# Hybrid mLSTM and pooling trunk: sums of z weight quarters of the pool input projection formed in device memory by accumulating DMAs, in place of VectorE's additions

## The reference

```python
def _pool_branch(x, w_in, w_group, scale, w_out):
    proj = x @ w_in                 # 1024x1024 @ 1024x4096
    u = proj[..., :E_B]             # E_B = 2048
    z = proj[..., E_B:]
    ...
    pooled = (jnp.concatenate(means, axis=-1) - uf).astype(x.dtype)   # moving means of u, windows 2, 4, 8, 16
    mixed = jnp.einsum("bsgc,gcd->bsgd", pooled, w_group).reshape(B, S, E_B) * scale
    return (mixed * jax.nn.silu(z)) @ w_out
...
x = _layer_norm(DEEPNORM_ALPHA * x + branch(x), post_ln_g[i], post_ln_b[i])
```

## Time and profile before

| | before |
|---|---|
| median of 3 runs | 1450.5 us (1450.19 to 1453.4) |
| span of the profiled execution | 1451.6 us |
| TensorE busy | 1433.7 us (99%) |
| VectorE busy | 1035.0 us (71%) |
| ScalarE busy | 767.7 us (53%) |
| GpSimd busy | 58.7 us (4%) |
| moved by DMA | 141.99 MB |

### The profile page before, as it was taken

One profiled execution on the slowest core, in us unless ns is written; L12 is line 12 of the kernel. 1 busy time (PEld: TensorE's weight loads), 2 busy tenths in 40 slices (PEclk: granted clock), 3 DMA queues, 4 the chain that ended last, 5 costly groups with the idle time before them and its releaser, 6 DMA issues.

```text
span 1451.6 us, 19237 instructions
## 1 busy us (share of the span) xinstructions
PE 1433.7 (99%) x6680; PEld 1192.7 (82%) x6680; DVE 1035.0 (71%) x1634; ACT 767.7 (53%) x1209; POOL 58.7 (4%) x125
## 2 busy tenths in 40 slices
PE   9999999999999999999999999999999999999997
PEld 7788888888888888888888888878888888888886
DVE  7978878797887879787734133677788777796515
ACT  6876757667576757658633234574444444442201
POOL 2001000000001000000000000000000000000001
PEclk9999999999999999999999999999999999999999
DMA  5022122131222203135473333441222222463121
GB/s 221 24 68 95 52 67 74 49 102 45 98 62 73 73 30 102 59 134 207 126 247 102 91 97 101 138 122 54 80 87 88 74 87 88 136 270 104 42 88 58
DMA packets 67360, 141.99 MB, mean 98 GB/s; under 512 B 6065, under 2 KB 32945, under 8 KB 66625
## 3 DMA queue, kind: packets, MB, share of 16 engines
q1 hardware_dynamic: 67264, 140.77, 29.6%
HBM read 111.32 MB, written 29.43 MB: 97 GB/s over the span
## 4 chain that ended last, share of the span: by engine, by line
PE 92%; ACT 4%; DVE 2%; DMA 1%; issue 1%; SPq 0%; POOL 0%; DVEq 0%; ACTq 0%; POOLq 0%
PE wide L2678 20%; PE wide L2680 20%; PE wide L2679 20%; PE ps_state L2678 3%; PE ps_state L2680 3%; PE ps_state L2679 3%; PE ps_inter L2679 2%; PE ps_inter L2678 2%; PE ps_inter L2680 2%; PE ps_intra L2850 2%; PE ps_state L2856 2%; PE ps_intra L2853 2%; PE ps_intra L2679 1%; PE ps_s L2679 1%; PE ps_intra L2678 1%; PE ps_s L2678 1%
## 5 line engine op out<-in xcount | busy, mean ns | idle before, releaser
L2679 PE MATMUL wide<-xa,inb 128*128 128x512 f32 x576 | 224.5, 390 | 0.0
L2678 PE MATMUL wide<-xb,inb 128*128 128x512 f32 x472 | 189.7, 402 | 0.9
L2680 PE MATMUL wide<-xb,inb 128*128 128x512 f32 x472 | 184.3, 390 | 0.0
L2679 PEld LDWEIGHTS wide<-xa,inb 128*128 128x128 f32 x576 | 108.4, 188 | 19.9
L2679 PE MATMUL wide<-xa,blk 128*128 128x512 f32 x320 | 124.5, 389 | 0.0
L2678 PEld LDWEIGHTS wide<-xb,inb 128*128 128x128 f32 x472 | 88.8, 188 | 20.2 <-issue 3.7
L2680 PEld LDWEIGHTS wide<-xb,inb 128*128 128x128 f32 x472 | 88.6, 188 | 18.9
L2680 PE MATMUL wide<-xb,blk 128*128 128x512 f32 x256 | 99.6, 389 | 0.0
L2678 PE MATMUL wide<-xb,blk 128*128 128x512 f32 x256 | 99.6, 389 | 0.0
L2678 PE MATMUL wide<-xa,inb 128*128 128x512 f32 x208 | 83.3, 400 | 4.2 <-ACT z_buf L1084 2.9
L2680 PE MATMUL wide<-xa,inb 128*128 128x512 f32 x208 | 81.2, 390 | 0.0
(11 more groups left out here) (436 smaller groups left out, 3826.8 us busy)
## 6 DMA issues: line engine op xcount, KB each, us to landing
in_raw<-in_w_in SPq DMA_DIRECT2D x45, 512.0 KB, 3.9
y_heads<-f_buf SPq DMA_DIRECT2D x32, 256.0 KB, 3.3
wm_raw<-in_w_out SPq DMA_DIRECT2D x16, 512.0 KB, 6.4
a_raw<-in_pool_w_z SPq DMA_DIRECT2D x16, 512.0 KB, 3.7
a_raw<-folded SPq DMA_DIRECT2D x16, 512.0 KB, 3.7
y_rows<-zz SPq DMA_DIRECT2D x16, 512.0 KB, 2.7
wo_raw<-in_pool_w_out SPq DMA_DIRECT2D x16, 512.0 KB, 7.7
ym_raw<-y_heads SPq DMA_DIRECT2D x32, 192.0 KB, 2.5
```

What stands on the lines that cost most here:

```text
L2678: pe.matmul(dst, a[0], b[0], start=first, stop=False, skip_group_check=more)
L2679: pe.matmul(dst, a[0], b[1], start=False, stop=False, skip_group_check=more)
L2680: return pe.matmul(dst, a[1], b[0], start=False, stop=last, skip_group_check=more)
```

## The change

The weights of z come in another layout: four parts, each [128, 8, 512] (`by_part` in place of `by_pair`), so that a part of all eight z pairs is one block of 2 MiB. Four arrays `z_sums[7]`, `[6]`, `[3]`, `[5]` of 2 MiB are added in device memory. GpSimd forms them with eight DMAs of its own, `z_step(0)` to `z_step(7)`, one at the end of each head: four plain copies within device memory (steps 0, 2, 4, 6) and four that add a part onto what is there (steps 1, 3, 5, 7). Each waits for the one before (`z_summed`). In the pool layer the 7 z pairs from p = 2 on take their sums from there: SyncE loads them (`load_sum`, four loads of 256 KB a pair) and no longer loads part 2. VectorE's four additions of these pairs go (28 in all); pair 0 and the u pairs keep theirs. The number of the semaphore for the gate weights is changed too (`gw_placed` becomes two more counts of `const_set`), with the same waits.

```diff
+Z_SUMS = (7, 5, 6, 3)
+Z_STEPS = 8
+def summed_on_chip(p):
+    return p % 2 == 1 or p == 0
...
+            def load_sum(p, q):
+                if q == 3:
+                    if p == 2:
+                        sp.wait_ge(added, 4)
+                    sp.wait_ge(blk_lo, AT[p - 2, 3] + 1)
+                else:
+                    sp.wait_ge(prod, AT[p, q] - RING + 1)
+                if p == 2 and q == 3:
+                    sp.wait_ge(z_summed, 16 * Z_STEPS)
+                dst = a_part(p, 2) if q == 3 else blk_sum_at(AT[p, q])
+                src = z_sums[q].rearrange("(c n) f -> c (n f)", n=2)[:, p // 2 * HALF:(p // 2 + 1) * HALF]
+                sp.dma_start(dst, src).then_inc(z_sum_in[q], 16)
...
-            for p in range(PAIRS - 2):
-                load_a(p + 2, 0)
-                if p >= 3 and p % 2:
+            for p in range(PAIRS):
+                if p and p % 2 == 0:
+                    for q in (6, 7, 5):
+                        load_sum(p, q)
+                if p < PAIRS - 2:
+                    load_a(p + 2, 0)
+                    if p % 2 == 0:
+                        load_sum(p + 2, 3)
...
+            def z_step(n):
+
+                part = [p_z[a, :, :, :].rearrange("c (m k) f -> (c m) (k f)", m=2) for a in range(4)]
+                dst, src, adds = ((7, part[0], False), (7, part[2], True), (6, z_sums[7], False), (6, part[3], True),
+                                  (3, z_sums[6], False), (3, part[1], True), (5, part[2], False), (5, part[3], True))[n]
+                if n:
+                    pool.wait_ge(z_summed, 16 * n)
+                if adds:
+                    pool.dma_start(z_sums[dst], src, accum_op=ALU.add, max_dma_last_dim=8192).then_inc(z_summed, 16)
+                else:
+                    pool.dma_start(z_sums[dst], src, max_dma_last_dim=8192).then_inc(z_summed, 16)
...
                 for f in range(2):
                     power(h, f)
+                z_step(h)
...
-                if (p, q) in AT and q == 5 and p + 1 < PAIRS:
+                if q == 5 and p + 1 < PAIRS and summed_on_chip(p + 1):
                     for part in (7, 6, 3):
                         add(p + 1, part)
-                elif q == 1 and p:
+                elif q == 1 and p and summed_on_chip(p):
                     add(p, 5)
```

More of the change, by code:

```diff
@@ L183, in a_loads, with sums_before @@
     return 16 * ((1 if p % 2 else PAIRS_A - 1) + p // 2 + 1)
+def summed_on_chip(p):
+    return p % 2 == 1 or p == 0
+def sums_before(p):
+    return 4 * (p // 2 + 1) if p else 0
 def by_vector(n):
@@ L208, in build @@
     folded = nc.dram_tensor("folded", (P, PAIRS // 2, 2, 2, 4, P), F32, kind="Internal").ap()
+    z_sums = {q: nc.dram_tensor(f"z_sum{q}", (2 * P, 4 * HALF), F32, kind="Internal").ap() for q in Z_SUMS}
     y_heads = nc.dram_tensor("y_heads", (ET, P, S), F32, kind="Internal").ap()
@@ L431, in build @@
         gw_in = sem("gw_in")
-        gw_placed = sem("gw_placed")
+        z_summed = sem("z_summed")
         bias_in = sem("bias_in")
@@ L552, in build @@
         late_in = y_in[4]
+        z_sum_in = dict(zip(Z_SUMS, (xt_in[1], xt_in[2], xt_in[3], xt_in[4])))
         wg_late_in = gw_in
@@ L587, in block_raw @@
             p, q = PRODUCTS[i]
-            return a_part(p, {1: 0, 2: 1, 3: 1, 4: 3}[q]) if q < 5 else blk_sum_at(i)
+            return a_part(p, {1: 0, 2: 1, 3: 1 if summed_on_chip(p) else 2, 4: 3}[q]) if q < 5 else blk_sum_at(i)
         def is_u(p):
@@ L737, in load_a @@
                     sp.wait_ge(blk_lo, AT[p - 2, 4 if j else 3] + 1)
-                src = folded[:, p // 2, j, :, :, :] if p % 2 else p_z[p // 2, :, j, :, :, :]
-                sp.dma_start(a_raw[:, p % 2, 2 * j:2 * j + 2, :],
-                             src.rearrange("c h t f -> c h (t f)")).then_inc(a_in[p % 2][j], 16)
+                parts = slice(2 * j + (j if not summed_on_chip(p) else 0), 2 * j + 2)
+                src = (folded[:, p // 2, j, :, :, :].rearrange("c h t f -> c h (t f)") if p % 2
+                       else p_z[parts, :, p // 2, :].rearrange("a c f -> c a f"))
+                sp.dma_start(a_raw[:, p % 2, parts, :], src).then_inc(a_in[p % 2][j], 16)
+            def load_sum(p, q):
[10 more added lines that the diff above has]
+                sp.dma_start(dst, src).then_inc(z_sum_in[q], 16)
             def store_y(k):
@@ L853, in _ @@
                             load_wm(k)
-            for p in range(PAIRS - 2):
-                load_a(p + 2, 0)
-                if p >= 3 and p % 2:
+            for p in range(PAIRS):
[6 more added lines that the diff above has]
+                        load_sum(p + 2, 3)
+                if 3 <= p < PAIRS - 2 and p % 2:
                     store_y(p - 2)
-                load_a(p + 2, 1)
-                if p >= 2 and p % 2 == 0:
+                if p < PAIRS - 2:
+                    load_a(p + 2, 1)
+                if 2 <= p < PAIRS - 2 and p % 2 == 0:
                     store_y(p - 2)
@@ L957, in _ @@
                 link(pool, pool.tensor_copy(g_raw[:, :, at], g_packed[:, :, n * HEADS:(n + 1) * HEADS]),
-                     gw_placed, n + 1)
+                     const_set, CONST_SETS + n + 1)
             n = 0
@@ L1227, in high_gates @@
             def high_gates():
-                act.wait_ge(gw_placed, 2)
+                act.wait_ge(const_set, CONST_SETS + 2)
                 link(act, act.activation(g_split[:, :, 0:P // 2], g_raw[:, :, :], ACT.Copy), gw_hi, 1)
@@ L1566, in block_hi @@
                     act.wait_ge(a_in[p % 2][1], a_loads(p))
+                elif not summed_on_chip(p):
+                    act.wait_ge(z_sum_in[q], 16 * (p // 2) + 16)
                 else:
-                    act.wait_ge(added, 4 * p + {7: 1, 6: 2, 3: 3, 5: 4}[q])
+                    act.wait_ge(added, sums_before(p) + {7: 1, 6: 2, 3: 3, 5: 4}[q])
                 if i >= RING:
@@ L2383, in block_lo @@
                 dve.wait_ge(blk_hi, i + 1)
-                if q in (6, 7):
-                    dve.wait_ge(added, 4 * p + {6: 3, 7: 2}[q])
+                if q in (6, 7) and summed_on_chip(p):
+                    dve.wait_ge(added, sums_before(p) + {6: 3, 7: 2}[q])
                 dve.tensor_tensor(blk_lo_at(i), block_raw(i), blk_hi_at(i).bitcast(F32), ALU.subtract
@@ L2399, in add @@
                     dve.wait_ge(prod, AT[p, q] - RING + 1)
-                link(dve, dve.tensor_tensor(dst, a, b, ALU.add), added, 4 * p + n)
+                link(dve, dve.tensor_tensor(dst, a, b, ALU.add), added, sums_before(p) + n)
             def prepare(i):
@@ L3096, with by_part @@
 _KEEP_LAYER_AXIS = ("mlstm_b_i", "mlstm_b_f", "post_ln_g", "post_ln_b")
-def by_pair(w):
-    return w.reshape(2, 4, P, PAIRS // 2, 2, P).transpose(3, 2, 4, 0, 1, 5)
+def by_part(w):
+    return w.reshape(2, 4, P, PAIRS // 2, 2, P).transpose(4, 0, 2, 3, 1, 5).reshape(4, P, PAIRS // 2, HALF)
 def by_head(w):
@@ L3152 @@
         "w_qkv": query_key_value(one["mlstm_w_q"], one["mlstm_w_k"], one["mlstm_w_v"]), "w_out": one["mlstm_w_out"],
-        "pool_w_z": by_pair(w_pool[:, E:]), "pool_w_u": unit_weights(w_pool[:, :E]),
+        "pool_w_z": by_part(w_pool[:, E:]), "pool_w_u": unit_weights(w_pool[:, :E]),
         "pool_w_g": group_weights(one["pool_w_group"]), "pool_w_out": one["pool_w_out"],
```

## The result

| | before | after |
|---|---|---|
| median of the runs | 1450.35 us (1450.05 to 1453.4, 4 runs) | 1465.78 us (1463.14 to 1467.55, 4 runs) |
| ratio | | 1.0102, 95% interval 1.0088 to 1.0117 |
| span of the profiled execution | 1451.6 us | 1463.7 us (own time 1465.57) |
| moved by DMA | 141.99 MB | 164.28 MB |

The change makes the kernel 15.4 us slower. The forecast was 1451.0 us, no change, with a range up to 1464: wrong, and outside the range.

The account below looks back on a forecast made before the run. TensorE, busy 1433.7 of 1451.6 us, was taken to bound the kernel. Additions 0, pool layer's loads 0, GpSimd's queue 0 and heads 0.5 us, on 1450.5, gave 1451.0 us, range 1448.5 to 1464.

Parts of the forecast that it names:

- VectorE and the pool layer: Pool layer: VectorE loses 19.3 us of additions, TensorE gains 0 us, and the added loads cost 0 us.
- rival 2: Pool layer: loads of sums come late, SyncE's queue having 21 more issues; 1 us lost per z pair makes 1458; chance 0.03.
- GpSimd's queue: Heads: issuing the steps on GpSimd costs 0 us; even 20 us of it would be hidden before the mask's first reader.
- The copies: Heads: a 2.10 MB copy moves in 6.3 us, ends at 389.6 and is gone before the close load.
- The accumulation's length: Heads: an accumulation was put at twice a copy, 12.6 us, ending at 395.9; bounded above by 25 us.
- the prediction's last sign: Profile after: an accumulation well over 12.6 us from issue to landing would make the prediction wrong.
- Rival 1: Heads 1, 3, 5: accumulations hold up the loads; 1453.8 us at 12.6 us and served last, 1466 to 1479 at 25; chance 0.31.
- If the engines give both transfers the same share ... 1.6 us late: Heads 1, 3, 5: the load's 1.6 us of moving become 3.2, under the 2.7 us margin, so nothing is lost.
- an accumulation of 25 us: Heads: upper bound with a slow adder; load 8 to 12 us late, 15 to 28 us lost in three heads.
- Served last of all: Heads 1, 3, 5: a load served last is 3.8 us late and costs 1.1 us a head, 3.3 in all: 1453.8 us.
- The load may be 0.5 + 0.2 + 2.0 = 2.7 us late before TensorE stops: Heads: margin before `sum_t`, idleness between, and margin of product 5's lower half; beyond it each us costs one.
- the nearest loads have more time: Mix: step 7's accumulation runs there, not beside the heads' close load, and no loss was counted for it.

Follow-up runs that it names:

- pool_only: Changed kernel without the eight z_steps, loading plain quarters of z's weights in place of the sums in the pool layer: 1450.93 us, ratio 1.0007 to the kernel before.
- load_ahead: Changed kernel with SyncE issuing the second half of pair 3h+2 ahead of the two y_heads stores that stood before it: 1461.39 us, ratio 1.0075.
- snap_first: Changed kernel with ScalarE's copy of product 1 of pair 3h+2 out of its bank put ahead of the two tanh of z: 1457.6 us, ratio 1.0046.
- last_add: Changed kernel with only step 7 accumulating, the other three accumulating steps made plain copies: 1453.38 us, ratio 1.0017.
- steps_only: Kernel before with the eight z_steps added on GpSimd, on arrays that nobody reads, VectorE keeping all additions: 1464.17 us, ratio 1.0097.
- whole_4k: Changed kernel with each accumulation one transfer in 4 KB pieces, of 240 of the 256 rows: 1463.04 us, ratio 1.0088.
- halves_8k: Changed kernel with each accumulation split in two transfers of 1 MB in 8 KB pieces: 1462.15 us, ratio 1.0073.
- late_step: Changed kernel with steps 0 to 6 issued 13 us later, behind the landing of the load that had been late: 1464.15 us, ratio 1.0091.
- pieces_4k: Changed kernel with each accumulation split in two transfers of 1 MB in 4 KB pieces: 1450.32 us, ratio 1.0004.

## Why the prediction was wrong

**VectorE and the pool layer: right.** 28 x 0.69 = 19.3 us of additions were to go, 17.4 went, and TensorE got none of it; `pool_only` confirms 0, within its interval, for the additions, the loads and SyncE's longer queue together (28 issues more, 7 pairs by 4, not the 21 of rival 2). **GpSimd's queue: right**, its issue took 0.94 us and the mask still starts at 388.17, long before its reader. **The copies: right**, 6.3 us estimated, 6.5 to 6.9 moving (8.9 in head 2), no loss.

**The accumulation's length: right.** 12.6 us was the estimate; in head 3 its large pieces moved from 387.4 to 399.8, 12.3 us. From issue to landing it was 15.5, and 15.0 were expected with the 2.4 us of fixed time; the prediction's last sign, "well over 12.6 us from issue to landing", left those 2.4 us out and so tells nothing. Rival 1 named the mechanism, the place (heads 1, 3, 5) and the load. It had 0.31, and my forecast 0.60 rested on three steps that failed.

**"If the engines give both transfers the same share ... 1.6 us late".** The share is one piece for one piece, and a piece of the accumulation takes 0.63 us, one of the load 0.16 by the packet records. I had applied this only to an accumulation of 25 us ("pieces that take several times as long"), while at 12.6 us it holds as well. Then there was what the sum left out: a store of SyncE's ahead of the load, whose pieces alternate too, and without it (`load_ahead`) 2.4 us more until the queue's first piece moves. The load was 4.2 us late in head 3 and 5.0 in heads 1 and 5. "Served last of all", 3.8 us late, was closer, and still a little short.

**"The load may be 0.5 + 0.2 + 2.0 = 2.7 us late before TensorE stops".** I followed VectorE's queue to product 5 and no other. TensorE stopped at product 6, for ScalarE's copy out of the bank. That chain was in the trace of before: ScalarE rests 1.33 us before it rounds `sum_t`, and then works without a pause up to the copy, which TensorE takes with 0.14 us of gap. So behind `sum_t` there were 1.3 us and not 2.2, and with the 0.6 us by which the load landed ahead of it (4.2 us late, 3.6 waited) the margin was 1.9 us and not 2.7. The queue that I did follow was read right: in `snap_first`, with the copy out of the way, TensorE loses 1.23 + 0.56 = 1.8 us behind a wait of 3.75, the second time at that very operand, so it had 2.0. ScalarE's timeline of the kernel before:

```profile
399.25 0.63 ACT L1060 ACTIVATE inb<-sum_t 128x512 fp32r<-128x512 f32 x1 [1.33 <-PE wide L2680]
...
400.58 0.63 ACT L1110 ACTIVATE o_buf<-z_buf 128x512 f32<-128x512 f32 x1
401.25 0.60 ACT L1077 ACTIVATE o_buf<-wide 128x512 f32<-128x512 f32 x1
```

VectorE's 3.6 us less 1.3 are the 2.3 us by which TensorE was later in head 3. By VectorE's three waits, 3.8, 3.6 and 4.5 us, less 1.3 each, the term that the sum had at 0 is 8.0 us (7.9 measured), and the time 1458.5.

**The mix: "the nearest loads have more time".** They had not: the stores and loads of `y_heads` follow each other there, each took 9 to 13 us beside step 7, and 2.8 us were lost (2.4 in `last_add`).

**The clock** was not in the sum: two of the three gaps were followed by 3.4 us at 1.2 GHz, 1.6 us each. Whether a gap is followed by one isn't settled by its length: over the seven traces in which a load of the heads was late (changed kernel, `steps_only`, `whole_4k`, `halves_8k`, `load_ahead`, `late_step`, `snap_first`) 13 of 18 gaps of 2.0 to 4.2 us in the heads were, and neither of the two of 1.2 to 1.3 us; but the wait of 1.28 us in the kernel before was the earlier trace rows, and the same wait in the changed kernel wasn't.

7.9 + 2.8 + 3.2 = 13.9 us, beside 13.8 for the median of `steps_only`. The medians of the change and of before differ by 15.4; the profiled execution has 1.6 us more at its start, where the change does nothing. That the change's four runs share this is not shown.

## What to carry to other kernels

A transfer that nobody waits for isn't free: here loads issued beside one landed about when it did, and in the mix, where several stood in SyncE's queue, up to 6 us later. So a long one goes where no load is issued that would be read before it ends, here a stretch of 15 us that cost nothing for the same bytes. The margin of a load is the smallest over all the engines that stand behind its first reader, banks to be emptied included, and not that of the operand it becomes. And an experiment that brings the time back may have changed more than its name says: `pieces_4k` did it by a pause, which only a second kernel without it could tell.

## What the runs showed of the hardware

An accumulating DMA within device memory took about twice a copy's time: 272 packets for 2.10 MB at a share of 59.6% of 16 engines over 18 us against 35.8% over 14 us, 0.67 and 0.31 us for each of the 256 large pieces (0.63 in their median). Halving the piece halved its time (0.33 us in `whole_4k`) and not the transfer's (13.2 us of moving in head 3 for 15/16 of the bytes, beside 12.3). GpSimd was held 9.14 us at the issue of a second accumulating transfer of 1 MB in head 3 of `halves_8k`, and not at all in heads 1 and 5 of the same execution; in `pieces_4k` it was held 8.7 to 10.6 us in all four steps. The queue's rows of the changed kernel for step 3 (384 to 402 us) and for step 2, a copy (304 to 318 us):

```profile
q0 software_dynamic: 272, 2.10, 59.6%
...
q0 software_dynamic: 272, 2.10, 35.8%
```
